# Moving two of eight modulation groups per layer from the delta-rule stage into layer norms

## The reference, cut to what matters

```python
for l in range(DEPTH):
    mix = hybrid_mixer(x, ...)
    x = layer_norm(DEEPNORM_ALPHA * x + mix, ln_mix_g[l], ln_mix_b[l])
    ff = swiglu(x, ...) if l % 2 == 0 else moe_swiglu(x, ...)
    x = layer_norm(DEEPNORM_ALPHA * x + ff, ln_ffn_g[l], ln_ffn_b[l])
...
silu_c, silu_cc = jax.nn.silu(c), jax.nn.silu(c_ctx)
for i in range(DEPTH):
    sh1, sc1, g1, sh2, sc2, g2 = jnp.split(silu_c @ ada_w[i] + ada_b[i], 6, axis=-1)
    csh1, csc1, cg1, csh2, csc2, cg2 = jnp.split(silu_cc @ ada_w[i] + ada_b[i], 6, axis=-1)
```

## Time and profile before

| | us |
|---|---|
| median of 3 runs (lowest, highest) | 3209.21 (3207.38, 3211.71) |
| time of the profiled execution | 3211.39 |
| span of its profile | 3209.6 |
| PE busy, share of the span | 2898.3 (90%) |
| DVE busy | 1566.6 (49%) |
| ACT busy | 1042.7 (32%) |
| mean granted clock of PE, share of 2.4 GHz | 0.956 |
| median to landing of a 1 MB load of the modulation weights | 4.8 |

### The profile page before, as it was taken

One profiled execution on the slowest core, in us unless ns is written; L12 is line 12 of the kernel. 1 busy time (PEld: TensorE's weight loads), 2 busy tenths in 40 slices (PEclk: granted clock), 3 DMA queues, 4 the chain that ended last, 5 costly groups with the idle time before them and its releaser, 6 DMA issues.

```text
span 3209.6 us, 67924 instructions
## 1 busy us (share of the span) xinstructions
PE 2898.3 (90%) x26308; PEld 1889.0 (59%) x26308; DVE 1566.6 (49%) x5142; ACT 1042.7 (32%) x2748; POOL 0.2 (0%) x4
## 2 busy tenths in 40 slices
PE   8979999977888888888888887988999999899998
PEld 7748887856455555555555555444444444556887
DVE  5551004564467676767676773774322210354331
ACT  3121002221455545555545542253211100243210
POOL 0000000000000000000000000000000000000000
PEclk9979999997999999999999998999999999999999
DMA  5543443473599999999999981100122212211441
GB/s 202 210 196 122 154 141 109 142 279 105 166 323 324 326 328 321 320 319 323 326 321 325 323 298 70 66 27 27 53 79 79 79 67 78 79 53 53 147 153 67
DMA packets 205858, 576.06 MB, mean 179 GB/s; under 512 B 6496, under 2 KB 6624, under 8 KB 179040
## 3 DMA queue, kind: packets, MB, share of 16 engines
q1 hardware_dynamic: 205536, 571.72, 51.7%
HBM read 570.65 MB, written 1.05 MB: 178 GB/s over the span
## 4 chain that ended last, share of the span: by engine, by line
PE 60%; DMA 22%; DVE 12%; issue 2%; ACT 2%; DVEq 1%; SPq 1%; ACTq 0%
PE P L491 44%; DMA ring<-ws_moe 20%; PE P L888 4%; DVE arena L1826 4%; DVE ring L1826 2%; DMA ring<-ws_b 2%; PE P L667 1%; PE P L574 1%; PE P L584 1%; DVE small L1478 1%; DVEq L1823 1%; PE P L593 1%; PE P L652 1%; PE P L856 1%; PE P L542 1%
## 5 line engine op out<-in xcount | busy, mean ns | idle before, releaser
L491 PE MATMUL P<-arena,ring 128*128 128x256 f32 (+1 forms) x2784 | 902.9, 486 | 22.7 <-ACT arena L1123 22.7
L491 PEld LDWEIGHTS P<-arena,ring 128*128 128x128 f32 x2784 | 534.2, 192 | 381.5 <-issue 336.1
L888 PE MATMUL P<-arena 128*32 128x256 f32 x6496 | 369.3, 380 | 5.5 <-DVE Y L1804 2.6
L888 PE MATMUL P<-ring,arena 128*32 128x256 f32 x4256 | 281.3, 415 | 90.0 <-DMA ring<-ws_moe 77.9
L491 PE MATMUL P<-X_sb,ring 128*128 128x256 f32 x1504 | 335.2, 385 | 3.9 <-ACT X_sb L1102 3.9
L491 PEld LDWEIGHTS P<-X_sb,ring 128*128 128x128 f32 x1504 | 289.6, 194 | 45.2 <-issue 5.3
L1826 DVE COPY arena<-ring 128x256 f32 x1120 | 234.9, 292 | 157.1 <-DMA ring<-ws_moe 142.5
L888 PEld LDWEIGHTS P<-arena 128*32 128x32 f32 x6496 | 214.3, 110 | 142.9 <-DVE ring L1826 8.0
L888 PEld LDWEIGHTS P<-ring,arena 128*32 128x32 f32 x4256 | 148.0, 119 | 209.1 <-DMA ring<-ws_moe 90.9
L1826 DVE COPY arena<-arena 128x256 f32 x1120 | 234.2, 292 | 66.9 <-DMA arena<-ws_moe 49.0
L1323 ACT ACTIVATE arena<-ring 128x256 f32 x560 | 181.9, 403 | 231.7 <-DMA ring<-ws_moe 170.4
(11 more groups left out here) (360 smaller groups left out, 2598.7 us busy)
## 6 DMA issues: line engine op xcount, KB each, us to landing
ring<-ws_moe SPq DMA_DIRECT2D x84, 2048.0 KB, 13.1
arena<-ws_moe SPq DMA_DIRECT2D x84, 2048.0 KB, 13.9
ring<-ws_b SPq DMA_DIRECT2D x137, 1024.0 KB, 4.8
ring<-ws_a SPq DMA_DIRECT2D x67, 1024.0 KB, 5.0
cst_sb<-cst SPq DMA_DIRECT2D x1, 1664.0 KB, 8.5
X_sb<-xT SPq DMA_DIRECT2D x1, 1024.0 KB, 4.9
X_sb<-ctxT SPq DMA_DIRECT2D x1, 1024.0 KB, 4.7
out<-Y SPq DMA_DIRECT2D x2, 512.0 KB, 2.6
```

The costliest lines, as they stand in the source:

```text
L491: ins = nc.tensor.matmul(bank(i, n), blockap(s, b % SLOT), rhs(kk), start=kk == 0, stop=kk == k - 1)
L888: ins = nc.tensor.matmul(acc(g // 2)[BR * j:BR * (j + 1), g % 2], x[:, b * BR:(b + 1) * BR], weights_of(b), start=k == 0, stop=last and kk ...
```

## The change

`ORDER` now names the groups: 0 to 5 of a layer stay ahead of its `out`, group 6 of layer 0 lies between `out0` and `up0`, group 7 between `down0` and `in1`, groups 6 and 7 of layer 1 between `out1` and the experts. On PE, groups 0, 1, 2 stand in levels 1, 3, 5 and groups 3, 4, 5 in chunks 0, 1, 2 of the scan; levels 2 and 4 have none. `linear_normed` takes the groups that it holds: three steps of k of the first between the sum of the mean and the variance, the rest behind the variance. ACT copies their rows behind its root; PE turns them behind the first tile of `up0` or `in1`, or behind the router's transposes; DVE writes `mod`, and PE waits for that (`mod_ready`) before it writes the bank again. The experts' first load also waits for all 16 groups.

```diff
-ORDER = ["in0", "ada0", "out0", "up0", "down0", "in1", "ada1", "out1", "moe",
+ORDER = ["in0", "ada0:0:6", "out0", "ada0:6:7", "up0", "down0", "ada0:7:8", "in1", "ada1:0:6", "out1", "ada1:6:8", "moe",
...
             sp.wait_ge(sem("tile_done"), TILE["out1"] + 8)
+            sp.wait_ge(sem("ada_done"), 16)
...
                 mean_of(y1, KD - 1)
+                b = (TILE[name] + KD - 2) % NBANK
+                if groups:
+                    ada(groups[0], 0, 3, b, 0)
                 variance()
+                for n, g in enumerate(groups):
+                    ada(g, 0 if n else 3, KD, b, n)
...
-                tiles_in(0, 3)
+                tiles_in(0, 1)
+                if l:
+                    ada_flip(P0[:, (TILE["in1"] + 2) % NBANK], 1, 0)
+                tiles_in(1, 2)
+                if l:
+                    C.take("mod_ready")
+                tiles_in(2, 3)
...
-                    ada(lev - 1, 0, 3)
+                    if lev % 2:
+                        ada(lev // 2, 0, 3, lev // 4, lev // 2 % 2)
...
-                    ada(lev - 1, 3, KD)
-                    if lev in (3, 5):
-                        ada_flip(lev // 2 - 1)
+                    if lev % 2:
+                        ada(lev // 2, 3, KD, lev // 4, lev // 2 % 2)
+                    if lev == 4:
+                        ada_flip(P0[:, 0], 2, 0)
...
-                linear_normed(f"out{l}", KD, lambda k: mix1[:, k, :])
+                linear_normed(f"out{l}", KD, lambda k: mix1[:, k, :], groups=(6, 7) if l else (6,))
                 if l == 0:
-                    linear("up0", 2 * KF, KD, lambda k: x1[:, k, :], T, ready=x_wait)
+                    linear("up0", 1, KD, lambda k: x1[:, k, :], T, ready=x_wait)
+                    ada_flip(P0[:, (TILE["up0"] + 2) % NBANK], 1, 0)
+                    linear("up0", 1, KD, lambda k: x1[:, k, :], T, first=1)
+                    C.take("mod_ready")
+                    linear("up0", 2 * KF - 2, KD, lambda k: x1[:, k, :], T, first=2)
...
                         ins.then_inc(sem("x_flipped"), 1)
+                    ada_flip(P1[:, 3], 2, 2)
                     C.take("picked")
...
                 a.activation(rstd[:, 0:T], P1[:, 1, 0:T], ACT.Sqrt, bias=ln_eps, scale=1.0 / D).then_inc(sem("ln_std"), 1)
+                if rows:
+                    ada_rows(*rows)
                 for k in range(0, KD, 2):
...
                 tokg = tok.rearrange("p (g d) -> p g d", d=HD)
+                if l:
+                    modulation(P0[:, (TILE["in1"] + 2) % NBANK], 0, 7, 1)
                 conv4(0)
...
                     L(v.tensor_tensor(rt[:, 64:66], mx[1], mx[0], ALU.subtract), "top_diff")
+                    modulation(P1[:, 3], 1, 6, 2)
                     V.take("top_exp")
```

More of the change, by code:

```diff
@@ L74, in plan @@
             continue
+        if ":" in name:
+            name, first, last = name.split(":")
+            array, at = source[name]
+            for g in range(int(first), int(last)):
+                slot[name, g] = len(src)
+                done += 1
+                src += [(array, at + 3 * g + j) for j in range(3)]
+                free += [("ada_done", done)] * 3
+            continue
         n, k = size[name]
@@ L78, in plan @@
         src += [(array, at + j) for j in range(slots)]
[L79 to L85, removed]
+        tile[name] = t
+        free += [("tile_done", t + min(n * k - 1, SLOT * j + SLOT - 1) // k + 1) for j in range(slots)]
+        t += n
     return tile, slot, src, free, source["a"], source["b"]
@@ L655, in chunks @@
                     return ins
[L657 to L675, removed]
-                        ins = nc.tensor.transpose(P0[:, b, 96 * q:96 * q + 96], ADR[0:96, b % 2, q * P:(q + 1) * P],
-                                                  c_("ident")[0:96, 0:96])
-                    ins.then_inc(sem("ada_flipped"), 1)
-                tiles_in(0, 3)
+                tiles_in(0, 1)
[5 more added lines that the diff above has]
+                tiles_in(2, 3)
                 C.take("decay_in")
@@ L815, in _ @@
                 C.take("delta_read")
-                C.take("mod_ready", 2 * NBANK)
+                C.take("mod_ready", 6)
                 attention(FOX_PAIRS,
@@ L848, in _ @@
                     C.take("x_rows", 2)
+                    C.take("mod_ready", 2)
                     C.take("row_map")
@@ L1459, in wide_norm, with modulation @@
                 V.take("x_even", KD // 2)
+            def modulation(turned, layer, first, n):
+                V.take("ada_flipped")
+                for g in range(n):
+                    m = 6 * (first + g)
+                    L(v.tensor_tensor(mod[:, layer, m:m + 6, :].rearrange("p (j h) c -> p h j c", h=2),
+                                      turned[:, 192 * g:192 * g + 192].rearrange("p (h j r) -> p h j r", h=2, j=3)[:, :, :, 0:2],
+                                      bc(v_(f"adab{layer}", m, 6).rearrange("p (j h) -> p h j", h=2).unsqueeze(3), [P, 2, 3, 2]),
+                                      ALU.add), "mod_ready")
             def gb(ap, c):
@@ L1623, in _ @@
                 taps(11, 17)
-                def modulation(b):
-                    V.take("ada_flipped")
-                    for g in range(2):
-                        m = 12 * b + 6 * g
-                        L(v.tensor_tensor(mod[:, l, m:m + 6, :].rearrange("p (j h) c -> p h j c", h=2),
-                                          P0[:, b, 192 * g:192 * g + 192].rearrange("p (h j r) -> p h j r", h=2, j=3)[:, :, :, 0:2],
-                                          bc(v_(f"adab{l}", m, 6).rearrange("p (j h) -> p h j", h=2).unsqueeze(3), [P, 2, 3, 2]),
-                                          ALU.add), "mod_ready")
                 for lev in range(1, 6):
@@ L1716, in _ @@
                 if l == 0:
+                    modulation(P0[:, (TILE["up0"] + 2) % NBANK], 0, 6, 1)
                     for m in range(KF):
```

70 lines of the change are left out of this document (46 added, 24 removed).

## The result

The changed kernel takes 3192.11 us (median of 6 runs, 3188.04 to 3199.54). The kernel before took 3211.31 us beside it (6 runs, 3207.38 to 3218.31). The ratio is 0.9941, 95% interval [0.9925, 0.9957]. That is faster by 19 us; the forecast was faster by 12, and 3192.11 lies in its range. The run of the profile took 3191.41 us, with a span of 3189.6.

What follows compares the result with a forecast made beforehand. PE, busy 90% of the span, was taken as the bound. Terms -8.1 - 7.2 - 1.4 + 2.3 + 2.4 = -12.0 gave 3199.4 against the profiled execution, 3197.2 against the median; range 3190 to 3203.

Steps and rivals of the forecast that it cites:

- What bounds the stage: Delta-rule stage, layer 0: nothing on PE is hidden in levels 1 to 4; a removed group saves 3.70 us.
- The rival that had the groups hidden there: Rival, chance 0.09: DVE needs about 7.5 us of a level, PE waits for it in levels 2 and 4; 3209, no change.
- the slower one: Rival, chance 0.04: small gaps in the thinned delta-rule stage let the clock fall; 3245, with the groups alone 3215.
- Layer 0, -8.1: Delta-rule stage, layer 0: scan begins 9.5 us earlier, PE waits 3.6 for a load, stage ends 8.1 us earlier.
- PE has finished level 5's products [...] and waits 1.1: Level 5, layer 0: PE finishes at 154.1, DVE's last convolution taps at 155.1, so PE waits 1.1 us for them.
- With the 11.3 of rows 1 the weights are there: Scan, layer 0: slots free at 168.0, weights there 11.3 us later at 179.3, a latency taken from the inversion.
- Layer 1, -7.2: Delta-rule stage, layer 1: 72.4 us before, now as long as layer 0's 65.2, so 7.2 us earlier.
- The clock: Scans of both layers: low clock behind the 3.6 us load wait; the bound, clock kept, gives -17.9 instead of -15.3.
- Norm behind out0, -1.4: Behind out0: group 6 fits into PE's waits at no cost, the clock is kept at up0; 1.4 us gained.
- Start of layer 1, +2.3: Ahead of tile 2: PE waits for DVE's mod of group 7, resumes at 536.6; 2.3 us lost.
- Behind out1, +2.4: Behind out1: later ACT scaling and router +1.5, transposes and mod on DVE's path +0.9; 2.4 us lost.
- The experts' first load, cost none: Experts' first load leaves at 782, not 769.4; loads end near 811, first product at 825.4, 14 us of cover.

Runs made afterwards that it cites:

- the first pair: The first profiled executions of the kernel before and the changed kernel, no further edit; first measurement 3192.11 us against 3211.31, ratio 0.9941.
- the repeat: Both kernels measured and profiled again with no edit: changed kernel 3194.68 us, ratio 0.9958; kernel before 3212.31 us, ratio 1.0011.
- The kernel with seven terms left out: Changed kernel with groups 6 and 7 cut to the last of their eight product steps, loads, copies, turns and writes kept: 3200.44 us, ratio 0.9979.
- The early modulation: Changed kernel with DVE's write of mod for group 7 put ahead of the attention's decay instructions in layer 1: 3196.22 us, ratio 0.9958.
- all three edits: Changed kernel with all convolution taps ahead of level 1, group 5 behind the scan, group 7's modulation ahead of DVE's decay: 3185.61 us, ratio 0.9929.

## Why the prediction was right

- **What bounds the stage.** Right. Removed matmuls in levels 2 and 4 were removed time; level 2 took what its products take. The rival that had the groups hidden there is out, and so is the slower one: the clock is 1.00 from 122 to 163 us. Only in layer 1 it fell once in the inversion, behind a wait of 2.16.
- **Layer 0, -8.1.** Measured -8.1 and -11.6. That the first is exact is luck: two errors cancelled. The step "PE has finished level 5's products [...] and waits 1.1" names the wrong wait: PE stopped for its code, 1.81 us, and DVE had the taps ready at 149.19 + 5.17 = 154.4, before PE needed them at 155.5. With the smaller stop in level 3 this put the scan's start 1.4 us behind the forecast, counted from the stage's start. "With the 11.3 of rows 1 the weights are there" was mis-sized: 10.0. So "PE waits 3.6" came to 1.97: PE reached group 5 1.7 us late (53.7 us behind the stage's start, forecast 52.0), and the weights came just when forecast (55.7). The low clock behind the wait came, 2.74 us for 18 instructions.
- **Layer 1, -7.2.** Measured -4.9 and -7.4. The step that failed is "the new stage is as long as layer 0's": in the first pair it was 2.3 longer, and the scan started 2.3 later behind the stage's start, 42.3 us for 40.0. The stops for code were longer, 2.16 and 0.65 (1.81 and 0.20 in layer 0), and the first brought the low clock to the two pieces behind it, 1.6 us. With the repeat the term is right within the scatter.
- **The clock.** I took it as low behind the load's wait in both layers. It was low in the first execution of the changed kernel; in the repeat group 5's first part ran at 1.50 us behind waits of 1.66 and, in layer 1, 2.27. That is the bound I had kept. It is 1.6 of the 2.2 us by which layer 0's stage is shorter in the repeat; the other 1.3 of the pair's difference come from the kernel before, whose stage was that much longer there.
- **Norm behind out0, -1.4.** Measured -1.4 and -1.8, by the mechanism named. The kernel with seven terms left out shows it from the other side.
- **Start of layer 1, +2.3.** Measured +2.3 and +2.2, but the step "PE resumes at 536.6" made all of it a wait, and the wait was 1.14 us. The rest is the tile ahead, which ran in part at the low clock, 5.84 us, and the two transposes. The early modulation took the wait away, and 0.75 us was all that came back. The number is luck, the wait is real.
- **Behind out1, +2.4.** Measured +2.2 and +0.6, with other parts. ACT's longer copy and the router gave +0.4 (forecast +1.5), the modulation on DVE +0.3 (+0.9), and the gather's products +1.5, which fell into a stretch of low clock in that execution and not in the repeat (there the parts were -0.1, +0.7 and 0). ACT's copy and scaling did end later, but the router's 32 instructions then ran as one piece in 5.21 us.
- **The experts' first load, cost none.** Right: its issue is at 768.97 us, 46 us ahead of the first expert product.
- **The size of the whole.** The forecast was -12. Traces up to the first expert product say -10.6 and -16.2, the medians -19 and -18, and the ratio of the second measurement -13.5. What lies behind that product took 2374.8 to 2392.5 us over fourteen traces, a scatter of more than any term of this sum; the range had room for it only because its bounds came from the clock. That both medians fell into it is in part luck.

## What to carry to other kernels

Where work is taken out of a stretch of small matmuls, ask next what else has to come per instruction. Here PE's own code did: 16 KB for some 127 small matmuls (two stops lie 255 apart), and a run of 64x64 products went through a piece in about 4.1 us (192 in 6.19). A wait marked "issue" in the middle of a run without a semaphore, always at the same count of instructions, is the sign of it; shifting the code by a few instructions tells it from a wait for data. Ask of a load that PE waits for when it could be issued: here group 5's loads go out when the scan's first group is done and PE has them 9.9 to 11.4 us later, so whatever delays the scan delays them too, and a stop ahead of them isn't hidden by their wait. In every execution of the changed kernel or an edit of it that kept group 5 in the scan and had full clock behind the wait, the stage ended 23.6 to 23.8 us behind the scan's start, which lay between 39.4 and 41.4 us. And take a latency from the same place of the trace, not from another stage. Work put into a wait ahead of a norm's end can be worth more than its cover, since it also keeps the clock.

## What the runs showed of the hardware

- PE stops for its own code. The stops of over 0.8 us in layer 0's inversion end 2.2 to 2.5 us after the start of a piece on queue 8, whose own packet takes about 1.0 us. In the kernel before they are there too, but smaller: in the repeat of it PE waits for "issue" twice in that stage, 1.5 us together.

```profile
PE P L652 <- issue: 1.5, 2, 1.0
```

- When a piece is asked for, and why the one at 149.87 us starts only then, stays open. A burst of weights (145.0 to 154.7 us) is under way at that moment, and pieces came 7.4 to 8.4 us apart in such bursts and 3.5 us apart around their ends; that the piece queues behind the weights fits this, but no run here held the weights back, so it isn't shown.
- The length of an idle stretch doesn't by itself tell what the clock does. Behind 2.67 us of it, it stayed at 1.00; behind 2.27 in the scan of layer 1 in the changed kernel's repeat 18 instructions took 1.50; behind 1.88 in level 5 of layer 1 with all three edits 18 instructions took 1.50; behind 2.16 at the same place of the changed kernel they took 2.55, behind 1.97 and 2.12 in the scans 2.74 and 2.55, and behind 2.09 the clock was 0.53.
